# A hybrid decoder step: where a token's norm factor is applied, and when a stage's first weights are loaded

## The reference

```
x += 0.5 * SwiGLU1(RMSNorm(x, g1))              # hidden width 2816
h  = RMSNorm(x, g_mix)
proj = h @ w_in                                  # short conv B, C, X; q, k, v; a, b; z; gates a, b
y_a = B * conv3(C * X)
y_b = gated DeltaNet(conv4+SiLU(q, k, v), a, b, z)   # 8 heads, per-token recurrence in chunks
x += (sig(gate_a) * (y_a @ w_a) + sig(gate_b) * (y_b @ w_b)) @ w_o
x += 0.5 * SwiGLU2(RMSNorm(x, g2))
return RMSNorm(x, g_final), and the convolution tails and recurrence states
```

## Time and profile before

| | us |
|---|---|
| median of 3 runs | 3563.65 |
| the profiled execution | 3570.27 |
| its span, first to last instruction | 3568.5 |
| TensorE busy | 3359.5 (94%) |
| VectorE busy | 1117.5 (31%) |
| ScalarE busy | 1045.6 (29%) |
| GpSimd busy | 942.9 (26%) |
| mean granted clock of TensorE | 0.956 |

### The profile page before, as it was taken

One profiled execution on the slowest core, in us unless ns is written; L12 is line 12 of the kernel. 1 busy time (PEld: TensorE's weight loads), 2 busy tenths in 40 slices (PEclk: granted clock), 3 DMA queues, 4 the chain that ended last, 5 costly groups with the idle time before them and its releaser, 6 DMA issues. The chain is left out here.

```text
span 3568.5 us, 51417 instructions
## 1 busy us (share of the span) xinstructions
PE 3359.5 (94%) x20274; PEld 3261.3 (91%) x20274; DVE 1117.5 (31%) x1696; ACT 1045.6 (29%) x1545; POOL 942.9 (26%) x520
## 2 busy tenths in 40 slices
PE   6999999997999799999999999769997999999997
PEld 6999999996999799999999999749997999999996
DVE  4232223224556322232232222232323232223223
ACT  4111111113333344544355453220123111111112
POOL 3112111214223323333233331301234212211212
PEclk8999999998999899999999999569998999999998
DMA  3111111102232212112121210254412111111101
GB/s 122 48 35 48 46 41 41 47 18 83 68 97 86 79 50 66 56 60 62 56 80 49 66 56 32 58 170 153 149 36 65 42 41 47 43 45 41 44 21 51
DMA packets 274431, 222.74 MB, mean 62 GB/s; under 512 B 12043, under 2 KB 251787, under 8 KB 274289
## 3 DMA queue, kind: packets, MB, share of 16 engines
q1 hardware_dynamic: 273988, 220.56, 20.4%
q10 hardware_dynamic: 324, 0.41, 0.0%
HBM read 170.66 MB, written 50.28 MB: 62 GB/s over the span
## 5 line engine op out<-in xcount | busy, mean ns | idle before, releaser
L163 PE MATMUL ffn_bank<-ffn_h_hi,ffn_w_hi 128*128 128x368 f32 x2112 | 699.5, 331 | 40.9 <-DVE ffn_h_lo L428 33.6
L164 PE MATMUL ffn_bank<-ffn_h_lo,ffn_w_hi 128*128 128x368 f32 x2112 | 700.2, 332 | 0.0
L165 PE MATMUL ffn_bank<-ffn_h_hi,ffn_w_lo 128*128 128x368 f32 x2112 | 698.8, 331 | 0.0
L163 PE MATMUL mix_bank<-mix_h_hi,mix_w_hi 128*128 128x368 f32 x1752 | 638.2, 364 | 22.7 <-DVE mix_h_lo L1030 17.1
L385 POOL TENSOR_TENSOR ffn_w_lo<-ffn_w_raw,ffn_w_hi 128x1024 fp32r<-128x1024 f32 x132 | 315.0, 2395 | 1176.6 <-ACT ffn_w_hi L381 1176.6
L164 PE MATMUL mix_bank<-mix_h_lo,mix_w_hi 128*128 128x368 f32 x1752 | 581.3, 332 | 0.0
L165 PE MATMUL mix_bank<-mix_h_hi,mix_w_lo 128*128 128x368 f32 x1752 | 581.1, 332 | 0.0
L163 PEld LDWEIGHTS ffn_bank<-ffn_h_hi,ffn_w_hi 128*128 128x128 f32 x2112 | 399.2, 189 | 42.1 <-issue 42.1
L746 POOL TENSOR_TENSOR mix_w_lo<-mix_w_raw,mix_w_hi 128x1024 fp32r<-128x1024 f32 x73 | 199.5, 2733 | 775.2 <-ACT mix_w_hi L741 775.2
L165 PEld LDWEIGHTS ffn_bank<-ffn_h_hi,ffn_w_lo 128*128 128x128 f32 x2112 | 398.9, 189 | 0.0
L164 PEld LDWEIGHTS ffn_bank<-ffn_h_lo,ffn_w_hi 128*128 128x128 f32 x2112 | 398.8, 189 | 0.0
(11 more groups left out here) (292 smaller groups left out, 4459.7 us busy)
## 6 DMA issues: line engine op xcount, KB each, us to landing
mix_w_raw<-in_w_in SPq DMA_DIRECT2D x73, 512.0 KB, 6.1
ffn_w_raw<-in_ffn_w_gate SPq DMA_DIRECT2D x44, 512.0 KB, 3.8
ffn_w_raw<-in_ffn_w_up SPq DMA_DIRECT2D x44, 512.0 KB, 3.8
ffn_w_raw<-in_ffn_w_down SPq DMA_DIRECT2D x44, 512.0 KB, 3.5
scratch_qkv<-mix_out SPq DMA_DIRECT2D x24, 552.0 KB, 2.8
scratch_x<-g_x SPq DMA_DIRECT2D x8, 552.0 KB, 7.8
scratch_z<-turn_z_out SPq DMA_DIRECT2D x8, 552.0 KB, 2.8
scratch_sig_a<-turn_gate_out SPq DMA_DIRECT2D x8, 552.0 KB, 2.7
```

What stands on the lines that cost most here:

```text
L163: pe.matmul(out, w_hi, x_hi, start=first, stop=False)
L164: pe.matmul(out, w_hi, x_lo, start=False, stop=False)
L165: return pe.matmul(out, w_lo, x_hi, start=False, stop=last)
```

## The change

The factor leaves the multiplicand. Products take `x * g` (high part by ScalarE with the gain as its scale, low part by one VectorE operation), and 1/rms multiplies what comes out of PSUM:

- `ffn`: VectorE reads the gate bank with a product by `rstd`; ScalarE applies SiLU from SBUF; VectorE multiplies by `rstd` again for the up half, and then by the up bank.
- block 0 of the mixer: VectorE reads the banks with the product; the sigmoid reads SBUF. q, k, v: ScalarE copies as before, then GpSimd multiplies the row by `rstd`, and only then may VectorE's convolution start.
- delta turns: VectorE reads B with `rstd`, C with its square (`factor2`, X is then left alone), z and the gates with `rstd`, and ScalarE's SiLU and sigmoid follow in place.
- final stage: one number per token and partition (`root`) scales the copies out of PSUM.

`rstd` itself is made in the following stage, beside the first products (`Factor`): the sum over partitions, ln and exp leave the end of `ffn` and `merge_outputs`. GpSimd's clearing of `rstd` waits for its last use. The raw slots of the weights are one allocation for the whole kernel (`RawSlots`), and each stage issues the next one's first three blocks when its own blocks are split.

```diff
+class RawSlots:
+    SLOTS = 3
+    def load_ahead(self, sp, sources):
+        for k, src in enumerate(sources):
+            sp.dma_start(self.sb[:, k, :, :], src).then_inc(self.ahead[k], 16)
+        self.sent += 1
+    def take_over(self, sp, raw_loaded):
+        for k in range(self.SLOTS):
+            sp.wait_ge(self.ahead[k], 16 * self.sent)
+            sp.sem_inc(raw_loaded[k], 16)
+
+class Factor:
+    def sum(self, pe, bank, b):
+        pe.matmul(bank[:, 0:TH], self.ones, self.rstd[:, third(b)], start=True, stop=True).then_inc(self.summed, 1)
+    def log(self, act, bank, b):
+        if bank is not None:
+            act.wait_ge(self.summed, b + 1)
+        act.activation(self.rstd[:, third(b)], bank[:, 0:TH] if bank is not None else self.rstd[:, third(b)], ACT.Ln,
+                       bias=self.eps_col, scale=1.0 / D).then_inc(self.logged, 1)
+    def root(self, act):
+        for b in range(NB):
+            act.wait_ge(self.logged, b + 1)
+            act.activation(self.rstd[:, third(b)], self.rstd[:, third(b)], ACT.Exp, scale=-0.5).then_inc(self.ready, 1)
...
 transpose_inputs:
+            slots.load_ahead(sp, ahead)
...
-            copies(dve, 0, vec_out, 0, 2 * NJ + NHIST // 4)
+            copies(dve, 0, vec_out, 0, 2 * NJ)
+            dve.wait_ge(summed, NJ)
+            for g in range(2):
+                at = N_META + 4 * P * g
+                dve.tensor_copy(rstd[:, at:at + 4 * P], sums[g][:, :, :].rearrange("p a b -> p (a b)"))
+            dve.tensor_copy(rstd[:, 0:N_META], sums[2][:, 0, 0:N_META])
+            dve.tensor_copy(rstd[:, PT:T], sums[2][:, 0, N_META:tail_rows])
+            copies(dve, 0, vec_out, 2 * NJ, 2 * NJ + NHIST // 4)
...
 ffn:
-            gate_up(0, 0)
+            slots.take_over(sp, w.raw_loaded)
+            w.load(sp, 0, 0, 3, up_src(0, 0, 1))
...
+            if ahead is not None:
+                sp.wait_ge(w.lo_done, w.UNITS * GROUPS)
+                slots.load_ahead(sp, ahead)
...
-            pool.wait_ge(h_ready[0], KC // 2)
+            pool.wait_ge(mid_ready, 6 * GROUPS)
             nrm.clear(pool)
...
+            if partial:
+                for b in range(2):
+                    fac.sum(pe, sum_banks[b], b)
...
             for k in range(KC):
-                pe.wait_ge(h_ready[k % 2], k // 2 + 1)
+                if partial and k == KC // 2:
+                    pe.wait_ge(fac.logged, 1)
+                    fac.sum(pe, sum_banks[0], 2)
+                pe.wait_ge(h_ready, k + 1)
...
-            for k in range(KC):
-                act.wait_ge(h_scaled, k + 1)
-                act.copy(h_hi[:, k, :], hid[:, k % 2, :]).then_inc(h_hi_done, 1)
+            def h_high(k):
+                act.activation(h_hi[:, k, :], x[:, k, :], ACT.Copy, scale=gains[:, g_at, k:k + 1]).then_inc(h_hi_done, 1)
+            for u in range(2):
+                h_high(u)
+                w.split_hi(act, 0, 0, u)
+            for k in range(2, 5):
+                h_high(k)
+            for b in range(2):
+                fac.log(act, sum_banks[b] if partial else None, b)
+            for k in range(5, KC):
+                h_high(k)
+            fac.log(act, sum_banks[0] if partial else None, 2)
+            fac.root(act)
...
-                        act.wait_ge(gu_done, i * GU + (GU * g + 6 * a + b + 1))
-                        act.activation(hid[:, a, third(b)], bank[b][:, 0:TH], ACT.Silu).then_inc(bank_free[b], 1)
+                        act.wait_ge(bank_free[b], i * USES + (USES * g + a + 2))
+                        act.activation(hid[:, a, third(b)], hid[:, a, third(b)], ACT.Silu).then_inc(silu_done, 1)
...
             for k in range(KC):
-                dve.scalar_tensor_tensor(hid[:, k % 2, :], x[:, k, :], gains[:, g_at, k:k + 1], rstd[:, :],
-                                         ALU.mult, ALU.mult).then_inc(h_scaled, 1)
-                if k % 2:
-                    h_low(dve, k - 1)
+                dve.wait_ge(h_hi_done, k + 1)
+                dve.scalar_tensor_tensor(h_lo[:, k, :], x[:, k, :], gains[:, g_at, k:k + 1], h_hi[:, k, :].bitcast(F32),
+                                         ALU.mult, ALU.subtract).then_inc(h_ready, 1)
+            dve.wait_ge(fac.ready, NB)
...
+                    for b in range(NB):
+                        dve.wait_ge(gu_done, i * GU + (GU * g + 6 * a + b + 1))
+                        dve.tensor_tensor(hid[:, a, third(b)], bank[b][:, 0:TH], rstd[:, third(b)], ALU.mult).then_inc(bank_free[b], 1)
+                    for b in range(NB):
+                        dve.wait_ge(silu_done, i * 6 + (6 * g + 3 * a + b + 1))
+                        dve.tensor_tensor(hid[:, a, third(b)], hid[:, a, third(b)], rstd[:, third(b)], ALU.mult).then_inc(rescaled, 1)
...
 final_output:
+            for j in range(NJ):
+                n = P if j < 8 else NS * LS
+                mm = pe.matmul(sum_bank[0:n, j:j + 1], rstd[:, tokens(j)], ones[:, 0:1], start=True, stop=True, skip_group_check=True)
+            mm.then_inc(summed, 1)
...
+            gain(1)
+            act.wait_ge(summed, 1)
+            act.activation(root[:, 0:8], sum_bank[:, 0:8], ACT.Ln, bias=eps_col, scale=1.0 / D)
...
+            for k in (3, 5, 7):
+                gain(k)
+            act.wait_ge(logged, 1)
+            act.activation(root[:, 0:8], root[:, 0:8], ACT.Exp, scale=-0.5)
...
+            for k in range(0, KC, 2):
+                dve.tensor_scalar(y[:, k, :], x[:, k, :], gains[:, g_at, k:k + 1], None, ALU.mult).then_inc(scaled[0], 1)
+            dve.wait_ge(rooted, 1)
...
 mixer, projection loop, GpSimd:
             with pool.Fori(0, H) as i:
                 for j in range(3):
+                    row_sample = pre[:, j, GP + PT:GL].rearrange("p (s l) -> p s l", l=GP + LS)[:, :, GP:]
+                    pool.wait_ge(bank_free[2], i * 3 + (j + 3))
+                    pool.tensor_tensor(pre[:, j, GP:GP + PT], pre[:, j, GP:GP + PT], rstd[:, 0:PT], ALU.mult)
+                    pool.tensor_tensor(row_sample, row_sample, rstd[:, PT:T].rearrange("p (s l) -> p s l", l=LS), ALU.mult) \
+                        .then_inc(pre_scaled, 1)
                     w.split_lo(pool, i, 3, 4 + j)
...
 ScalarE at the mixer's start:
+            h_high(0)
             w.split_hi(act, 0, 3, 0)
+            for k in range(1, 5):
+                h_high(k)
+            for b in range(NB):
+                fac.log(act, a_banks[b], b)
+            fac.root(act)
+            for k in range(5, KC):
+                h_high(k)
...
+            act.activation(raw[2], raw[0], ACT.Sigmoid).then_inc(ab_sig, 1)
...
 VectorE, rates and convolution:
-            dve.wait_ge(ab_ready, 3)
+            dve.wait_ge(x_spilled, 16 * KC)
+            for b in range(NB):
+                dve.wait_ge(w.unit_done, b + 1)
+                dve.tensor_tensor(raw[0][:, third(b)], bank[b][0:2 * H, 0:TH], rstd[0:2 * H, third(b)], ALU.mult).then_inc(bank_free[b], 1)
...
+            dve.wait_ge(ab_sig, 1)
...
-                    dve.wait_ge(bank_free[2], i * 3 + (j + 3))
+                    dve.wait_ge(pre_scaled, i * 3 + (j + 1))
...
 delta turns, ScalarE and then VectorE:
+                    if g == 1:
+                        act.wait_ge(bank_free[b], h * 3 + (NQ + j + 2))
+                        ins = act.activation(gate_out[j][:, third(b)], gate_out[j][:, third(b)], ACT.Silu if j == 0 else ACT.Sigmoid)
...
+                    if g == 1:
+                        if b == 0:
+                            dve.wait_ge(gate_stored[j], i * 16 + 16)
+                        dve.wait_ge(w.unit_done, h * 9 + (NB * (NQ + j) + b + 1))
+                        dve.tensor_tensor(gate_out[j][:, third(b)], bank[b][:, 0:TH], rstd[:, third(b)], ALU.mult).then_inc(bank_free[b], 1)
+                    elif j < 2:
...
+                        dve.tensor_tensor((bb, cc)[j][:, third(b)], bank[b][:, 0:TH], (rstd, factor2)[j][:, third(b)], ALU.mult) \
+                            .then_inc(bank_free[b], 1)
```

More of the change, by code:

```diff
@@ L635, in _ @@
                 for c in range(4):
[L636 to L637 removed]
+                    mm = pe.transpose(bank[q % 6][0:n, c * P:(c + 1) * P], y[:, k + c, tokens(j)], ident[:, :])
                 mm.then_inc(turned, 1)
[L640 to L642 removed]
+        @block.scalar
```

256 lines of the change are left out of this document (111 added, 145 removed).

## The result

| | kernel before | changed kernel |
|---|---|---|
| median of the runs | 3563.84 us (3559.21 to 3566.44, 4 runs) | 3527.93 us (3526.61 to 3531.82, 4 runs) |
| profiled execution, its span | 3570.27 us, 3568.5 us | 3526.63 us, 3524.8 us |
| mean granted clock | 0.956 | 0.962 |

The ratio is 0.9901, 95% interval 0.9889 to 0.9913: 35.9 us faster, where 29.3 were forecast (3527.9 against 3534).

The account below looks back on a forecast made before the run. TensorE, busy 94% of the span, was taken as the bound, so gains lie only in its idles: 12.5 + 21 - 21.5 - 2.8 - 3 + 13.9 + 9.2 = 29.3 us off the median 3563.65 gives 3534, range 3522 to 3550.

Parts of the forecast that it names:

- start and sweep of the first feed-forward stage: First feed-forward stage: earlier first products 8.0, a ScalarE wait 2.8 and half clock 1.7 go; 12.5 us gained (9 to 15).
- first feed-forward stage to mixer: Handover to the mixer: block 1 starts 23 us sooner, less a wait of 2; 21 us gained (17 to 24).
- projection loop and last round: GpSimd's multiplication by 1/rms before the convolution delays TensorE: 21.5 us lost in the loop, 2.8 in the last round.
- delta turns: Delta turns: the extra VectorE read at the end of odd turns costs 7 x 0.45, 3 us lost (+3 to -15).
- merge to second feed-forward stage: Second feed-forward start: first products 8.1 sooner, a 4.5 wait and 1.8 half clock go; 13.9 us gained (11 to 16).
- final stage: Final stage: the factor chain leaves, 7.2, and the passes and copies out give 2; 9.2 us gained.
- the wait of 2: Mixer: TensorE, through with block 1 at 886, waits 2 us for per-head preparation ending near 888.
- every second round: Projection loop: half clock follows TensorE's 2.35 us wait in every second round, 1.7 x 3 = 5 us lost.
- the slack of 0.75: End of a projection-loop round: ScalarE's copy of bank 0 is done 0.75 us before TensorE needs it.
- none of it: 3512: Rival on the projection loop: the factor's 2.7 us do not reach TensorE; 3512 us, chance 0.2.
- much more: 3549: Rival on the projection loop: half clock every round and GpSimd's low part colliding with all taps cost 36; 3549, chance 0.15.
- The third rival: Delta turns: VectorE's 120 bank reads become the bound, costing up to 77 us; 3608 us, chance 0.06.

Follow-up runs that it names:

- that of the gate banks: Changed kernel with the delta turns' 120 gate and short-convolution banks read by ScalarE straight from PSUM, without 1/rms: 3527.33 us, ratio 0.9893 to the kernel before.

## Why the prediction was right, step by step

The measured column takes the means of the two traces of each kernel; by these the spans differ by 39.6 us (3566.3 and 3526.7), by the medians the times do by 35.9. The first step ends at GpSimd's last addition of squares, the step before the final stage at VectorE's last addition to x.

| step | forecast | measured |
|---|---|---|
| start and sweep of the first feed-forward stage | +12.5 | +12.7: 8.2 at the first product, 4.5 behind it |
| first feed-forward stage to mixer | +21 | +24.4 (22.9 to 25.8) |
| projection loop and last round | -24.3 | -23.3: 14.3 waits, 2.8 last round, 6.2 clock and rest |
| delta turns | -3 | +1, within the spread |
| merge to second feed-forward stage | +13.9 | +14.3: 8.5 (5.9 to 8.8) and 5.8 |
| steady feed-forward groups | 0 | 0.5 each, inside the stages' sums |
| final stage | +9.2 | +9.9 |

**First start: right.** Products came at 33.44, forecast 33.7. The chain ends as named, in GpSimd's second low part with a pass of h_lo in between, and is 8.26 us long where 8.1 were forecast. One link differs: the second low part did not start behind ScalarE's second high part (done at 29.39), but behind GpSimd's own first low part, at 29.97. Splitting the weights first starts that part sooner, and shortened the wait by 1.3 in this stage.

**Mixer: right in mechanism, short by 3 us.** Products came 5.7 us after the last addition (6.4 forecast) and block 1 at 859.80, 20.2 after it (21.3 forecast): 1.2 more of gain at that point. Two terms were mis-sized. The sigmoid was counted twice: in the 10.5 us of the preparation, which in the kernel before hold its table load and its pass, and once more in front of it.

```profile
895.13 1.28 ACT L1449 ACT_TABLE_LOAD   x1
...
896.42 1.18 ACT L1449 ACTIVATE g_x<-mix_bank 16x368 f32<-16x368 f32 x3
```

The preparation took 8.0 and ended 1.0 us before TensorE came, so the wait of 2 was none. And the gain was read at block 1's start (23), though block 1 ran partly at half clock in the first trace of the kernel before: 13.8 us, 12.2 in its second trace, 12.3 in the changed kernel. At block 1's end the gain is 25.8 by the first pair of traces. Of this 2.9 hang on a clock fall that the second trace of before doesn't have.

**Loop: right, and the term that mattered.** Seven waits of 2.04 (forecast 2.35), three clock falls (forecast three), 2.8 at the end (forecast 2.8). That the sum came within 1 us is in part luck: the waits were 2.2 less than forecast and the clock and rest 1.2 more, and "every second round" was a guess; the clock fell behind four of the same seven waits in another run. A wait of 2.14 and the slack of 0.75 make a chain 2.9 longer, where 3.1 were forecast: the factor takes 2.75 (2.44 + 0.31), but the 0.4 for low part and first tap product starting together did not come. First tap and three more take 7.1 us in the kernel before (the first one's 0.81, below, and the 6.28 of the earlier trace rows) and 7.12 after. The run without the factor gives all of it back (293.0), the run with two takes 32.6 more; both rivals on the loop (none of it: 3512; much more: 3549) fall.

```profile
974.04 0.81 DVE L1630 TENSOR_SCALAR mix_conv<-mix_pre,mix_gc_w 128x1128 f32<-128x1128 f32 x1 [4.16 <-ACT mix_pre L1474]
```

The rule that the prediction took from the Trainium skill (SBUF — State Buffer, Who interferes with whom) holds here for tensor_scalar too: the first tap product takes 0.81 us alone and 2.87 where GpSimd's low part started 0.14 before it, and with VectorE first it takes 0.81 and the later taps bear the wait.

**Turns: the step failed, at a price of about 4 us by the traces.** "There the extra VectorE read adds 0.4 to 0.6: 7 x 0.45": the waits for the mask did grow, by 2.7 (8.8 less 6.1), and fell by 1.9 when ScalarE read the banks again. But nothing of that is found in the length of the turns, which is 1017.4 to 1021.7 in nine traces with VectorE reading and 1019.6 in the one without, where 1024 and more were forecast. A wait that grew here did not lengthen its stage. What made up for it, and what moves the turns by 4 us with the same code in them, is open. The third rival (120 reads become the bound, 3608) falls with it.

**Second feed-forward stage: right** in both parts: 8.5 (forecast 8.1; with the same code in five of the other runs the stretch took 332.3 to 335.2 us, 341.1 before, so it is known to 2 us or so) and 5.8 (forecast 4.5 + 1.8 less the third sum's 0.5). **Final stage: right**, 9.9: 6.5 between VectorE's last addition and the first pass (7.2 forecast), 3.4 behind it (2 forecast). By the forecast's own boundary, GpSimd's last addition, the first of these is 7.5, and the 5.8 of the step before are 4.8.

The steps of the traces bring 10.3 us more than the 29.3 forecast: 4 from the turns, 3.4 from the mixer's start, 1 from the loop and the rest in small parts, 0.6 of it outside the steps. The medians bring 6.6 more. The two traced executions of the kernel before took 3568.0 us on average, where its medians are 3563.84 to 3566.05; one of them holds the clock fall of 2.9 us, so the traces overstate the gain, and how the 6.6 divide is not shown. The measured time, 3527.9, lies inside the forecast's own range, 3522 to 3550.

## What to carry to other kernels

When work goes from in front of a product to behind it, look for the engine queue in which its delay stands in front of something that TensorE needs: here 2.7 us on an idle GpSimd cost 23 us, and one line in ScalarE's queue, a copy put before a SiLU, gave 20 of them back without touching the work. Slack is counted once: a chain with 0.75 us to spare passes on everything above it, one to one. And take two traces of the same kernel before a step of 3 us is believed; two were too few for the turns here, which moved by 0.8 us in two traces of one kernel and by 2.7 in two of the other.

## What the runs showed of the hardware

- The granted clock does not answer to an idle alone. In four traces with the same seven waits in the loop, the half clock followed none of the four idles of 1.4 us and 13 of the 24 of 2.14 or 2.15: three in each trace, four in that of the weights asked for in the stage, and not always behind the same ones (the second, fourth and sixth in that of the gate banks). Of seven idles of 4.2 to 5.0 us it followed all. And the same mixer start ran at 0.50 in one execution and at 0.82 in another, which made the stretch 2.9 us longer or shorter.
- A tensor_scalar of 128x1128 on VectorE, 0.81 us alone, took 2.87 beside a GpSimd subtraction of 2.40 that had started first. Whichever of the two started first, the convolution with its first product took 7.1 us.
- GpSimd's multiplication of 128x1040 took 2.02 to 2.45 us for the same shape, its subtraction of 128x1024 took 2.40 alone and up to 3.6 beside VectorE.
